# Moving the split activations of a transformer kernel by some bytes in on-chip memory, and letting three scratch rows share a buffer

## The reference

```
x = layer_norm(ALPHA * x + rwkv7_time_mix(x, ...))
x = layer_norm(ALPHA * x + swiglu_ffn(x, w_in[0], w_down[0]))
x = layer_norm(ALPHA * x + attention(x, w_qkv, w_o))
x = layer_norm(ALPHA * x + swiglu_ffn(x, w_in[1], w_down[1]))
z = rmsnorm(x) @ w_in_2                      # conv, mLSTM, forgetting attention
x = x + concat(mlstm(z), forgetting(z)) @ w_out_2
x = x + cross_attention(rmsnorm(x), rmsnorm(mem)) @ w_xo
x = x + relu(rmsnorm(x) @ w_ff1)**2 @ w_ff2
return rmsnorm(x)
```

## The kernel before, in words

| buffer | before | mod 64 | after | mod 64 |
|---|---|---|---|---|
| `w_hi`, `w_lo` | 41088, 65664 | 0, 0 | the same | 0, 0 |
| `mix_hi`, `mix_lo` | 98432, 106624 | 0, 0 | the same | 0, 0 |
| `rx_hi`, `rx_lo` | 175904, 184096 | 32, 32 | the same | 32, 32 |
| `x_hi` | 118176 | 32 | 118928 | 16 |
| `x_lo` | 126368 | 32 | 128176 | 48 |
| `hid_hi`, `hid_lo` | 182400, 186496 | 0, 0 | 184448, 188544 | 0, 0 |

## Time and profile before

### The profile page before, as it was taken

The page is one execution under the profiler, slowest core; times in us unless marked ns, Lnnn a source line. Parts: engine busy times, 40 slices in busy tenths (PEclk is TensorE's granted clock), DMA queues, the critical chain, the costliest instruction groups (busy, mean ns, idle before and its releaser), DMA issues.

```text
span 1168.6 us, 24785 instructions
## 1 busy us (share of the span) xinstructions
PE 1141.0 (98%) x10550; PEld 1042.4 (89%) x10550; DVE 752.2 (64%) x1087; ACT 623.9 (53%) x916; POOL 119.5 (10%) x97
## 2 busy tenths in 40 slices
PE   7999999999999999999999999999999999999997
PEld 7798877789999989988999999899998898999996
DVE  7888886375554467897645445898587555555554
ACT  8974654454433446565634433675566564544443
POOL 0032263401100000220010000011000000000000
PEclk9999999999999999999999999999999999999999
DMA  8631111145554644434555447455434443655550
GB/s 302 226 108 48 55 57 56 61 163 195 195 195 157 244 180 174 151 109 145 180 217 188 179 172 252 147 178 197 164 129 148 158 144 126 217 188 178 211 179 36
DMA packets 29804, 187.30 MB, mean 160 GB/s; under 512 B 3472, under 2 KB 5648, under 8 KB 8592
## 3 DMA queue, kind: packets, MB, share of 16 engines
q1 hardware_dynamic: 27072, 177.21, 42.0%
q10 hardware_dynamic: 2640, 8.75, 2.3%
HBM read 184.90 MB, written 1.05 MB: 159 GB/s over the span
## 4 chain that ended last, share of the span: by engine, by line
PE 87%; DVE 6%; ACT 4%; issue 2%; DMA 0%; ACTq 0%; DVEq 0%; SPq 0%
PE ps L2125 25%; PE ps L2126 24%; PE ps L2127 24%; PE ps L2458 1%; PE ps L2453 1%; PE ps L2599 1%; PE ps L2262 1%; ACT mixed L639 1%; PE ps L2455 1%; DVE w_lo L1396 1%; PE ps L2347 1%; PE ps L2395 1%; PE ps L2846 1%; PE ps L2854 1%; ACT w_hi L745 1%
## 5 line engine op out<-in xcount | busy, mean ns | idle before, releaser
L1400 DVE TENSOR_TENSOR w_lo<-w_raw,w_hi 128x2048 fp32r<-128x2048 f32 x149 | 346.7, 2343 | 125.3 <-ACT w_hi L610 124.6
L2125 PE MATMUL ps<-x_hi,w_hi 128*128 128x256 f32 x1344 | 378.7, 282 | 4.3 <-DVE x_lo L1689 1.5
L2126 PE MATMUL ps<-x_lo,w_hi 128*128 128x256 f32 x1344 | 375.4, 279 | 0.0
L2127 PE MATMUL ps<-x_hi,w_lo 128*128 128x256 f32 x1344 | 375.2, 279 | 0.0
L610 ACT CAST w_hi<-w_raw 128x2048 fp32r<-128x2048 f32 x147 | 280.1, 1907 | 147.6 <-PE ps L2127 147.2
L2125 PEld LDWEIGHTS ps<-x_hi,w_hi 128*128 128x128 f32 x1344 | 252.8, 188 | 11.1 <-issue 4.7
L2126 PEld LDWEIGHTS ps<-x_lo,w_hi 128*128 128x128 f32 x1344 | 252.9, 188 | 1.3
L2127 PEld LDWEIGHTS ps<-x_hi,w_lo 128*128 128x128 f32 x1344 | 252.9, 188 | 0.0
L2125 PE MATMUL ps<-w_hi,hid_hi 128*128 128x512 f32 x304 | 118.8, 391 | 0.1
L2126 PE MATMUL ps<-w_lo,hid_hi 128*128 128x512 f32 x304 | 118.8, 391 | 0.0
L2127 PE MATMUL ps<-w_hi,hid_lo 128*128 128x512 f32 x304 | 118.4, 389 | 0.0
(11 more groups left out here) (419 smaller groups left out, 1782.3 us busy)
## 6 DMA issues: line engine op xcount, KB each, us to landing
w_raw<-in_weights SPq DMA_DIRECT2D x163, 1024.0 KB, 4.9
xt<-in_xT SPq DMA_DIRECT2D x2, 512.0 KB, 5.4
w_raw<-in_weights SPq DMA_DIRECT2D x2, 512.0 KB, 6.2
x_tm<-in_x SPq DMA_DIRECT2D x1, 1024.0 KB, 5.4
gain<-in_mix_g ACTq DMA_DIRECT2D x2, 512.0 KB, 5.1
gain<-in_mix_b ACTq DMA_DIRECT2D x2, 512.0 KB, 6.8
gain<-in_ffn_g ACTq DMA_DIRECT2D x2, 512.0 KB, 7.3
gain<-in_ffn_b ACTq DMA_DIRECT2D x2, 512.0 KB, 9.3
```

The source lines that it names most:

```text
L1400: V.tensor_tensor(w_lo[:, i % WS, :], w_raw[:, i % RAW, :], w_hi[:, i % WS, :].bitcast(F32), ALU.subtract).then_inc(lo_done, 1)
L2125: nc.tensor.matmul(out, hi_l, hi_r, start=start, stop=False)
L2126: nc.tensor.matmul(out, hi_l, lo_r, start=False, stop=False)
L2127: return nc.tensor.matmul(out, lo_l, hi_r, start=False, stop=stop)
```

## The change

`x_hi` and `x_lo` become slices of buffers that are 256 elements (1 KiB) larger, and begin 188 and 196 elements behind the start of these. All buffers that are allotted behind them move up by 1 or 2 KiB, a multiple of 64. To make room, `zf`, `za` and `ones_t` are no longer buffers of their own, but the first 12 partitions of the first three of the four key rows in `fx_k`; the buffers behind them move down by 1 KiB. Every engine's instructions, their order and their waits are those of before; only addresses differ.

```diff
+X_AT = (188, 196)
 LORA_B = GLORA - P
 ...
-        x_hi = sb("x_hi", [P, KT, T], F32R, a_m)
-        x_lo = sb("x_lo", [P, KT, T], F32R, a_m)
+        x_hi, x_lo = (sb(name, [P, KT * T + 256], F32R, a_m)[:, n:n + KT * T].rearrange("p (k c) -> p k c", k=KT)
+                      for name, n in (("x_hi", X_AT[0]), ("x_lo", X_AT[1])))
 ...
-            zf, za, ones_t, gi = (sb(n, [12, T], where=a) for n in ("zf", "za", "ones_t", "gi"))
+            gi = sb("gi", [12, T], where=a)
+            zf, za, ones_t = (fx_k[0:12, n, :] for n in range(3))
```

## The result

The changed kernel takes 1172.72 us (median of 13 runs, 1170.85 to 1175.96) against 1168.91 us for the kernel before (13 runs, 1168.22 to 1171.73). The ratio is 1.0031, 95% interval 1.0022 to 1.0040: slower, by 3.6 us by the ratio, where 14.8 us faster were forecast.

The account below looks back on a forecast made before the run. TensorE's matmul spacing was taken to bound the kernel: 4704 × 3.3 ns = 15.5 us, 95% of it 14.8 us, other parts 0, so 1168.6 − 14.8 = 1153.8, about 1154 us. The 8-in-10 range was 1138 to 1178.

Parts of the forecast that it names:

- That the spacing of the split matmuls sets the time: TensorE, busy 98% of the span: changes in the spacing of matmul starts change the end nearly one for one.
- That 4704 matmuls are in reach: 4032 matmuls with x moving and 672 with x stationary are touched, 47% of the span; each nanosecond is 4.70 us.
- the shared rows and other engines at 0: Key rows shared with zf, za and ones_t, and x's splits and casts on other engines: each counted as 0 us.
- That the excess follows the address: Split matmuls' time beyond their columns: 12.0 ns at remainder 0 from the weights, 8.7 and 9.3 ns at 32.
- The floor of 108 ns: Estimated need of 256 columns with nothing holding them, from plain float32 cross-score matmuls at 216 ns and half the rate.
- One more step of the size seen between 0 and 32, 3.3 ns less: Matmuls with x at 16 and 48 fall to 113.4 ns moving and 115.0 stationary, 15.5 us in sum; chance 0.42.
- the table of remainders modulo 64: Buffer addresses: mix shares the weights' remainder modulo 64, x and rx lie 32 bytes behind; the change puts x at 16 and 48.
- The rival on distance: Cost falls evenly from equal to opposite remainders, so x matmuls cost 1.65 ns more, 7.8 us slower, 1176.5 us; chance 0.27.
- The rival that nothing changes: For matmuls with x, remainders 16, 32 and 48 are alike once unequal to the weights'; 1169 us, chance 0.19.
- PE and ACT never wait on anyone: Skill rule cited against the forecast: taken strictly, x's start address costs TensorE nothing and the sum is zero.
- The forecast's 113.4 ns: Forecast spacing of the matmuls with x moving, 3.3 ns below 116.7.
- The deep case: Nearly the whole excess of the x matmuls goes, leaving 108 ns and a nanosecond or two: 31 us faster, 1138; chance 0.12.

Follow-up runs that it names:

- The run at 0: Changed kernel with x_hi and x_lo both 0 bytes behind the weights; ratio 1.0104 to the kernel before.
- The layout alone: Changed kernel with x_hi and x_lo back at remainder 32, larger buffers and shared rows kept; ratio 0.9999 to the kernel before.
- Equal halves at 16 and 48: Two runs of the changed kernel, x_hi and x_lo both 16 or both 48 bytes behind the weights; ratios 1.0042 and 1.0055 to the kernel before.
- 32 with 0: Changed kernel with x_hi 32 and x_lo 0 bytes behind the weights; ratio 1.0030 to the kernel before.
- 0 against 64 or 32 against 96: Changed kernel, both halves of x at 0, 64, 32 or 96 bytes behind the weights; ratios 1.0104, 1.0024, 1.0007, 1.0115 to the kernel before.
- 40: Changed kernel with x_hi and x_lo both 40 bytes behind the weights; ratio 1.0073 to the kernel before.
- 96, 128 and 160: Changed kernel with x_hi and x_lo both at 96, 128 or 160 bytes behind the weights; ratios 1.0115, 1.0091 and 1.0061 to the kernel before.
- 192: Changed kernel with x_hi and x_lo both 192 bytes behind the weights; 1168.91 against 1170.47 us, ratio 0.9989.
- 48 with 16: Changed kernel with its two values exchanged, x_hi at 48 and x_lo at 16; ratio 1.0003 to the kernel before.
- The two runs that moved the weights: Changed kernel with x at 48, w_hi and w_lo moved by 16: ratio 1.0077; kernel before with w_lo alone moved by 32: 1.0081.
- the run with the weights moved: Changed kernel with x_hi and x_lo at 48 and w_hi and w_lo moved by 16 bytes; ratio 1.0077 to the kernel before.

## Why the prediction was wrong

**That the spacing of the split matmuls sets the time: right.** TensorE is the chain, and the kernel follows the spacing by about nine tenths. The run at 0 shows it best: 4032 × (119.9 − 116.8) + 672 × (120.0 − 118.3) = 13.6 us by the spacings, 12.2 us by its ratio of 1.0104.

**That 4704 matmuls are in reach, and the shared rows and other engines at 0: right.** The layout alone has 0.9999, and VectorE's busy time in the changed kernel is that of before, 752.2 us.

**That the excess follows the address: right**, and confirmed by moving `x_hi` and `x_lo` together through eleven places, 116.6 to 120.0 ns. The floor of 108 ns under the excess is half the spacing of another kind of matmul and no run shows it; the shortest slab with `x` in any run had 113.3. So that the plain matmuls stream "without any excess" is not shown either.

**"One more step of the size seen between 0 and 32, 3.3 ns less": the step that failed.** It measured +0.85 ns moving and −0.46 ns stationary. Two things were wrong in it. First its direction: it took the distance from 0 to 32 as the start of a slope that goes on when the halves differ too. Equal halves at 16 and 48 have 118.4 ns, above 32's. Halves that start apart were the second reason. They did gain at 16 and 48, 0.7 ns against the equal halves and 1.7 ns the other way round, but not at 32 with 0, and never enough to come below the 116.7 of before. The change left the best place tried for `x` moving in the first net (32, or 288, which reads the same), for two that are each 1.6 ns worse. Second, its variable: the table of remainders modulo 64 set the whole argument, and 0 against 64 or 32 against 96 show that this isn't the variable. By the same table `rx` was the prediction's second witness at 32; modulo 256 it lies 160 behind the weights, where `x` costs 118.4 ns.

**The rival on distance had the direction, and was right on a number for a wrong reason.** Its 118.35 ns for 16 and 48 are the measured 118.4 of equal halves. But 40 costs 119.2 and not 117.6, and 96, 128 and 160 have no place in it; and its 1176.5 us stand against 1172.7 measured, because the mixed pair costs only half of that. The rival that nothing changes missed by 3.1 us in the spacings, and missed in time by as much as the one on distance, 3.7 against 3.8 us. The start address alone moved the same matmuls between 116.8 and 120.0 ns (32 and 96). The rule "PE and ACT never wait on anyone" of the Trainium skill (page "SBUF — State Buffer", section "Who interferes with whom") is about one engine waiting for another. The prediction stretched it to start addresses, and stretched so far it doesn't hold here; whether TensorE's two own reads wait for each other no run shows.

**The forecast's 113.4 ns exists, but not where it was forecast.** 113.3 ns was seen at another address (192), for a quarter of the slabs. That is luck: the prediction's reasoning doesn't lead to 192. The deep case's 109 or 110 ns was seen nowhere.

**What stays open.** Why 16 with 48 costs 117.7 and 48 with 16 only 116.7, when both alone cost 118.4. The period, 128 or 256. What puts a stream at 113 or at 118 ns. Why 40 costs 119.2. The two runs that moved the weights also moved other buffers; the weights' place counts beside that of `x`, as `w_lo` showed, but whether it is the difference or each address for itself isn't settled. For the difference speaks that 96 moving and 160 stationary, which are one difference modulo 256, have 120.0 and 119.9 ns. And how the hardware makes an address cost time: no run here shows it.

## What to carry to other kernels

When TensorE is the bound and each matmul has a load beside it, as here, the start addresses of the two buffers can be worth up to 3% of the matmul (116.7 to 120.0 ns in this kernel), so read the spacing of starts before and after any change of layout, even one that only adds a scratch row: three pads of 32 bytes cost this kernel 1.5%. Two measured phases don't make a slope; sweep the offset over at least 256 bytes in one buffer with the rest fixed. And before averaging a spacing, look at it slab by slab, since two stable values can hide in a mean.

## What the runs showed that I had not expected

- One address, two stable spacings: 113.3 ns over 132 matmuls and 117.8 ns 20 us later, `x` at 192, granted clock 1.00 in both.
- The 512-column matmuls are as sensitive as the others, and not at the same places: 227.7 ns with `hid` at 0, 233.8 at 96, and 233.2 in the run with the weights moved; with `mix` 228.4 at 0 and 233.1 at 32.
- 8 bytes more than 32 cost 2.4 ns (116.8 to 119.2).
- The effect is exactly repeated within a kernel: in the kernel before, round after round of the first two nets has 96 matmuls in 11.20 us, and at 0 the spacings are 120 ns nearly one by one.
